# First attention of a two-layer diffusion step: the value products of a head pair and query tile stand together in one head step instead of in two

## The reference, cut to what matters

```python
def block_attention(q, k, v, scale):
    def one_block(qblk):                      # 128 queries
        s = jnp.einsum('bqhgd,bkhd->bhgqk', qblk, k) * scale
        p = jax.nn.softmax(s, axis=-1)
        return jnp.einsum('bhgqk,bkhe->bqhge', p, v)
```

## Time and profile before

| | |
|---|---|
| time, median of 3 runs | 1373.82 us (1367.92 to 1375.38) |
| profiled execution | 1371.09 us, its span 1369.3 us |
| PE busy | 1256.3 us, 92% of the span |
| PEld busy | 660.8 us, 48% |
| DVE, ACT, POOL busy | 583.9, 418.2, 55.8 us |
| chain that ended last | PE 76%, SPq 8%, DMA 4%, DVE 4% |
| L1621, value products of the first attention | 52.4 us, x672 |
| mean granted TensorE clock | 0.967 of full speed |

### The profile page before, as it was taken

How to read it: one execution, slowest core, us unless ns; L and a number is a source line. 1 busy time by engine, 2 the same in 40 slices (tenths; PEclk the granted TensorE clock), 3 DMA queues, 4 the chain that set the end, 5 groups by cost and what they waited for, 6 DMA issues and landing times.

```text
span 1369.3 us, 16486 instructions
## 1 busy us (share of the span) xinstructions
PE 1256.3 (92%) x5449; PEld 660.8 (48%) x5449; DVE 583.9 (43%) x1334; ACT 418.2 (31%) x843; POOL 55.8 (4%) x64
## 2 busy tenths in 40 slices
PE   5899899999999999999939996999999999998884
PEld 2455566666664464444414443555444554443331
DVE  1322355444553664222236446677725642212215
ACT  2332344444451121111122336667621211111113
POOL 0102000000000120000020000000000100000002
PEclk9999999999999999999969997999999999999997
DMA  9969999422253067999970004000030469999945
GB/s 375 397 240 414 408 410 414 171 94 94 94 195 134 31 275 263 384 382 371 340 292 9 0 0 190 2 1 1 25 132 31 190 229 374 355 345 343 346 178 216
DMA packets 78545, 299.44 MB, mean 219 GB/s; under 512 B 11817, under 2 KB 29932, under 8 KB 62988
## 3 DMA queue, kind: packets, MB, share of 16 engines
q1 hardware_dynamic: 48096, 206.46, 41.1%
q0 software_dynamic: 16640, 64.56, 12.1%
q10 hardware_dynamic: 13740, 27.52, 5.5%
HBM read 223.79 MB, written 74.73 MB: 218 GB/s over the span
## 4 chain that ended last, share of the span: by engine, by line
PE 76%; SPq 8%; DMA 4%; issue 4%; DVE 4%; ACT 2%; ACTq 1%; DVEq 1%; POOL 1%; POOLq 0%
PE ps L1916 14%; PE ps L1588 10%; PE ps L1573 10%; PE ps L1528 8%; PE ps L1933 6%; PE ps L1806 6%; SPq L468 4%; PE ps L1769 4%; PE ps L1968 3%; PE ps L1621 3%; PE ps L1647 3%; PE ps L1871 2%; PE ps L1543 2%; DMA arena<-in_ada_w 2%; PE ps L1762 2%
## 5 line engine op out<-in xcount | busy, mean ns | idle before, releaser
L1916 PE MATMUL ps<-arena 128*128 128x512 f32 x560 | 246.2, 593 | 0.0
L1528 PE MATMUL ps<-const,arena 128*128 128x128 f32 (+2 forms) x1000 | 157.9, 286 | 58.3 <-DVE arena L1025 19.9
L1528 PEld LDWEIGHTS ps<-const,arena 128*128 128x128 f32 (+2 forms) x1000 | 118.4, 144 | 138.0 <-issue 34.8
L1077 DVE TENSOR_REDUCE hst<-ps 128x1 f32<-128x640 f32 (+1 forms) x160 | 114.7, 717 | 126.3 <-PE ps L1806 89.0
L1573 PE MATMUL ps<-arena 128*128 128x512 f32 (+2 forms) x400 | 156.3, 548 | 8.1 <-DVE arena L1036 4.8
L1916 PEld LDWEIGHTS ps<-arena 128*128 128x128 f32 x560 | 103.9, 190 | 117.2 <-issue 117.1
L690 ACT ACTIVATE arena<-ps 128x640 f32<-128x640 f32 (+1 forms) x160 | 98.9, 618 | 183.9 <-PE ps L1528 169.8
L1588 PE MATMUL ps<-arena 128*128 128x512 f32 x320 | 142.0, 597 | 1.4 <-issue 1.4
L1933 PE MATMUL ps<-arena 128*128 128x512 f32 x280 | 126.1, 593 | 2.2 <-ACT arena L789 2.2
L695 ACT ACTIVATE arena<-ps,hst 128x640 f32<-128x640 f32 (+1 forms) x160 | 112.6, 704 | 20.1 <-DVE hst L1077 19.9
L1573 PEld LDWEIGHTS ps<-arena 128*128 128x128 f32 x400 | 76.4, 195 | 81.6 <-issue 63.9
(11 more groups left out here) (201 smaller groups left out, 1102.0 us busy)
## 6 DMA issues: line engine op xcount, KB each, us to landing
arena<-in_ada_w SPq DMA_DIRECT2D x62, 768.0 KB, 11.4
slot_rows<-arena POOLq DMA_DIRECT2D x10, 4096.0 KB, 66.2
arena<-in_moe_w_down SPq DMA_DIRECT2D x35, 1024.0 KB, 17.8
arena<-in_moe_w_gate SPq DMA_DIRECT2D x31, 1024.0 KB, 9.2
arena<-in_moe_w_up SPq DMA_DIRECT2D x31, 1024.0 KB, 12.7
slot_rows<-arena ACTq DMA_DIRECT2D x35, 512.0 KB, 8.0
arena<-slot_rows SPq DMA_DIRECT2D x124, 128.0 KB, 11.4
arena<-in_moe_fed SPq DMA_DIRECT2D x8, 1024.0 KB, 9.5
```

The source lines that it names most:

```text
L1077: nc.vector.tensor_reduce(hst[:, b:b + 1], scores(s, step(s)[3]), AX.XY, ALU.max, negate=True)\
L1528: return nc.tensor.transpose(out, in_, ident[0:rows, 0:rows])
L1916: last = mm(split(bank(gu_bank(u)), 2), e_xsT[:, nth(u, D)][:, k * P:(k + 1) * P], w[:, k], start=k == 0, stop=k == KD - 1)
```

## The change

`pair` loses its argument `half`, computes all blocks of its tile in one loop, and is called in even steps only. In odd steps TensorE has no value products. No product is added, removed or changed.

```diff
-            def pair(p, half):
+            def pair(p):
                 m, it = divmod(p, NTILE)
                 blocks, first = (1, 5) if it == 0 else (LKEYS // P, 0)
-                js = (range(0, (blocks + 1) // 2), range((blocks + 1) // 2, blocks))[half]
-                if half == 0:
-                    pe.wait_ge(S("pt_ready"), 2 * p + 2)
-                    ...
-                for j in js:
+                pe.wait_ge(S("pt_ready"), 2 * p + 2)
+                ...
+                for j in range(blocks):
                     for odd in range(2):
                         last = mm(oT_out(it)[VD * odd:VD * (odd + 1)], v_of(2 * m + odd, first + j),
                                   ptbuf(2 * p + odd, blocks * P)[:, j * P:(j + 1) * P], start=j == 0, stop=j == blocks - 1)
-                if js and js[-1] == blocks - 1:
-                    last.then_inc(S("pv_done"), 1)
+                last.then_inc(S("pv_done"), 1)
...
                 if l:
                     wide(s)
-                elif s >= 4:
-                    pair((s - 4) // 2, s % 2)
+                elif s >= 4 and s % 2 == 0:
+                    pair((s - 4) // 2)
```

More of the change, by code:

```diff
@@ L1606, in heads @@
             g = l * STEPS
-            def pair(p, half):
+            def pair(p):
                 m, it = divmod(p, NTILE)
                 blocks, first = (1, 5) if it == 0 else (LKEYS // P, 0)
-                js = (range(0, (blocks + 1) // 2), range((blocks + 1) // 2, blocks))[half]
-                if half == 0:
-                    pe.wait_ge(S("pt_ready"), 2 * p + 2)
[L1615 to L1618, removed]
-                for j in js:
+                pe.wait_ge(S("pt_ready"), 2 * p + 2)
+                if it == 0:
+                    spare_free(0, m, PROMPT_AT)
+                if m and it == 1:
+                    pe.wait_ge(S("oT_latent"), m)
+                for j in range(blocks):
                     for odd in range(2):
```

## The result

In the first comparison the changed kernel took 1359.89 us in the median of 4 runs (1349.58 to 1371.7) and the kernel before 1370.87 (1367.78 to 1375.38), a ratio of 0.9888 with an interval of 0.9841 to 0.9935. The forecast was 1366.3 in 1361 to 1373: 7.5 us less, where the medians differ by 11 and the ratio says 15, since it leaves out the one launch of the changed kernel (1371.7) that lies over 1.5% above its fastest. Two further comparisons of the same two kernels gave 1.0003 (0.9943 to 1.0063) and 0.997 (0.9927 to 1.0013).

A forecast was written before the change was run, and what follows sets the result against it. TensorE alone was taken to bound nearly the whole first attention. Terms 7.0 + 1.1 - 0.1 - 0.4 - 0.1 = 7.5 us off the 1373.8 median gave 1366.3, in a range of 1361 to 1373.

The forecast's parts named there:

- The price of a group: First attention, TensorE: going from the full array to 64-column tiles and back costs 0.16 + 0.19 = 0.35 us.
- The steady pairs: First attention: a steady pair, from one `ada` of r = 9 to the next, takes 1.2 us less than 33.44.
- nearest miss: Key product at r = 0: ScalarE's copy ends 0.56 us after `ada`, the product starts 0.42 + 0.55 after it.
- Tile 2: Pairs 0 to 6, odd step ending with `ada`: each merge saves only 0.16 us, 7 x 0.16 = 1.1 us.
- Tile 4 of pair 6: Odd step r = 3 of the last pair, without hook: TensorE waits 0.4 us for VectorE; costs 0.1 us.
- The last pair's end: Last pair of the first attention: ten products of tile 2 instead of six before the last `ada`; costs 0.4 us.
- Rival (a): Odd steps with hooks: VectorE or ScalarE takes up the slack, 20 x 0.21 comes off, 1370.5; chance 0.12 with (e).
- Rival (b): 27 tiles: transposes wait for ScalarE's copy, put off by 0.43 us; 3.5 us slower, 1377; chance 0.04.
- Rival (c): Behind the first attention: something on its own clock, so the attention shortens but the time does not, 1374; chance 0.04.
- (d): Way back behind `ada` costs nothing, a merge is worth 0.38: 9.5 us, 1364.3; chance 0.80 together with the forecast.
- (e): All 27 merges: only the group's own 0.16 is saved, 3.7 us in all, 1370.1; chance 0.12 together with (a).
- The range: Whole time 1361 to 1373: from (d) less 3 us of spread to (a) and (e) with 3 us of spread.

The follow-up runs named there:

- best_home: Changed kernel with tile 2's value products in its odd step behind `ada`, the other tiles' in the even step; 1363.34 us, ratio 0.9953 to the kernel before.
- after_again: The changed kernel run again, unedited, against the kernel before; 1366.48 us in the median of 12 runs, ratio 1.0003.
- interleaved: Changed kernel with tiles 1 to 3 cut up, each block's products behind one of the even step's five transposes; 1391.12 us, ratio 1.0165 to the kernel before.
- switch_twice: Changed kernel with each latent tile's even-step products split, three blocks before the hook and two behind; 1367.37 us, ratio 1.0037 to the kernel before.
- best_last: As best_home, but tile 4 of pair 6 and tiles 1 and 3 of pair 7 also in their odd step; 1366.71 us in 6 runs.
- after_third: The changed kernel a third time, unedited, against the kernel before; 1365.53 us in 12 runs, ratio 0.997.

## Why the prediction was right or wrong

**The price of a group** (0.16 there, 0.19 back, nothing else computed) was right, in the changed kernel, with the groups doubled, and with three tiles of a pair cut into five; the way back costs 0.15 before transposes.

**The steady pairs** (1.21 us each) came out at 1.11. The step that failed is the overlap that the prediction called its nearest miss: that the key product at r = 0 would not wait for ScalarE's copy of `ada`'s result (L635). It takes 1.38 us instead of 1.29, and the wait is the cause. The timeline of the changed kernel, and below it the load of the kernel before, whose copy ended at 248.91:

```profile
243.60 0.49 ACT L635 ACTIVATE arena<-ps 128x384 f32<-128x384 f32 x1
...
244.32 0.94 PEld L1759 LDWEIGHTS ps<-arena 128*128 128x128 f32 x4
...
249.63 0.95 PEld L1762 LDWEIGHTS ps<-arena 128*128 128x128 f32 x4
```

The copy ended at 244.09 and the first weight load of the key product began 0.23 us later. In all eighteen steady pairs of the three profiles of the changed kernel this distance is 0.22 to 0.27 us, wherever the pair lies, while it is 0.7 in the kernel before and 1.4 in best_home, where the product takes 1.29 again. The prediction compared the end of the copy (0.56 us after `ada`) with the start of the product in the chain (0.97 after it). But the weight load stands ahead of that start. In the kernel before it begins 0.55 us after the first load of the transposes; here that would be at 244.23, 0.14 us after the copy, and it began 0.09 later, when the copy let it. So the 0.41 us of slack that the prediction's numbers imply were not there.

**Tile 2** at 0.16 and not 0.35 was right: scores behind `ada` keep 0.42, and best_home gets the other 0.19 by standing elsewhere. **Tile 4 of pair 6** waits for VectorE as said, 0.43 us; the cost was 0.3 and not 0.1, as the transposes behind the wait take 0.76 us instead of 0.55.

**The last pair's end** (0.4 us lost) is the term that was mis-sized. The prediction took ScalarE's issues to be as long as in its one profile. By its terms the last pair takes 24.9 us: the 25.2 of before, less 0.59 for pair 6's tile 2 and 0.25 for its tile 3, plus 0.1 for its tile 4 and 0.43 for the last pair's tile 2. Where the issues took 4.1 us (after_again) it came out at 25.3. Of the 0.4 between, 0.2 are the slower transposes of tile 4 just named, and 0.2 that TensorE's transposes came 5.09 us after the first issue instead of 4.87. Where the issues took 5.7, TensorE idled 2.7 us, went to the 1.2 GHz level, and the pair took 28.5 and 29.9. So in place of 0.3 us gained the last pair lost 0.1 in one profile, and 3.3 and 4.7 in the two others.

The fall of the clock does not follow from the length of the wait alone. Behind such a wait for ScalarE the granted clock fell to 0.50 after 1.6 us (interleaved), 2.1 (best_home), 2.7 and 2.7 (the changed kernel), and stayed at 1.00 after 2.6 (switch_twice) and 1.2 (after_again).

With all of tile 1's products behind the transposes of step r = 6, where the issues begin, six profiles have issues of 5.7, 5.7, 5.6, 5.1, 4.4 and 4.1 us; with six products there or none, nine profiles have 3.8 to 4.1. In interleaved they stand between those transposes, mostly ahead of the issues, and the issues take 3.8. So the length goes with a long group beside the issues, as best_last against best_home says too: it is one more thing that the merge brought. That is a coincidence in sixteen profiles and not a cause that was shown. Why an issue of ScalarE takes longer then, and by amounts that differ, stays open.

**Rival (a)**, a wait of 0.21 in every odd step, did not come: the wait is there once in a pair, at r = 5, as before. **Rival (b)** needed ScalarE's issues in the odd step to turn the sign; they are in one step of 80, and there they took back up to 4.6 us (after_third against after_again). **Rival (c)**, a later stage on a clock of its own, is out by the kernels without row transfers. **(d)** and **(e)** both fail on the chains above.

**The range** is where the forecast missed the median. Its step "with 3 us of spread" is the term that failed: it was set from three runs that lay 7.5 us apart. Across the comparisons launches of the kernel before lie between 1349 and 1383 us, with a standard deviation of 8. The median of four runs of the changed kernel fell 1.1 us outside, by the luck of those four: in 12 runs each, after_again and after_third had medians of 1366.48 and 1365.53, which lie inside. The centre was good: 7.5 us forecast; 5.7 measured where the scatter is out, 6.3 in the profiles of that pair, and 2.0 to 6.6 in the stage with the last pair as it falls. The chances, half for over 0.5%, were a little high, as the gain is about 0.4%. In two comparisons of three even the sign could not be told from the times.

## What to carry to other kernels

Where TensorE is the only piece of the chain, products that use part of the array's columns should stand together, and next to another change of tiles, such as `ada` here: count the groups, not the products, and read their price off as the length of a group less its instructions, and the excess of what follows. When instructions are moved together, look at what the emptied step had hidden: a copy that a later load waits for cost 0.09 us a pair here. In a step in which another engine issues DMAs and TensorE must wait for it, leave TensorE's list as short as it was; in four of the five profiles with a wait of 1.6 us or more the idle time cost more than itself through the clock. And before a gain of half a percent is timed, look for the stage that changes from run to run, and time the two kernels without it.

## What the runs showed of the hardware

- A change between the full array and 64-column tiles costs 0.16 us on the way there (behind `make` and transposes) and 0.15 (before transposes) to 0.19 (before scores and `make`) back. From `ada`'s 32-column tiles to 64-column tiles costs the same 0.16, and from them to the full array 0.19. The Trainium skill, TensorEngine Tiling (Array Packing), section Key Properties, has the rule that a change of the tiling mode drains the engine. The trace agrees in that every such change costs time; these are its figures.
- The same DMA issue on ScalarE (L730) took between 0.68 and 2.64 us in sixteen profiles with it in its place, and 8.60 and 8.90 when moved behind the loop.
- The second layer's expert stage took 196, 213 and 216 us in three executions of the changed kernel; with the row transfers left out it took 193.5 in all five profiles.
